# Four gathers of expert outputs, spread over the last item of a mixture-of-experts layer

## The reference

```
def moe_swiglu(h, router, w1, w3, w2):
    ...
    top_val, top_idx = lax.top_k(logits, TOP_K)          # two experts for each token
    gates = jax.nn.softmax(top_val, axis=-1)
    ...
    def one_block(args):
        xi, e = args
        return (jax.nn.silu(xi @ w1[e]) * (xi @ w3[e])) @ w2[e]

    yb = lax.map(one_block, (xb, block_e)).reshape(cap, D)
    out = jnp.zeros_like(t).at[slot_tok].add(yb * slot_g[:, None].astype(yb.dtype))
```

## Time and profile before

| | |
|---|---|
| median of three runs | 1869.29 us |
| the profiled execution's own time | 1876.34 us |
| its span | 1874.5 us |
| PE busy | 1820.3 us (97%) |
| DVE busy | 1383.7 us (74%) |
| ACT busy | 1119.5 us (60%) |
| POOL busy | 191.2 us (10%) |
| HBM read | 475.05 MB |
| DMA, whole span | 265 GB/s |

### The profile page before, as it was taken

How to read it: one execution, slowest core, us unless ns; L and a number is a source line. 1 busy time by engine, 2 the same in 40 slices (tenths; PEclk the granted TensorE clock), 3 DMA queues, 4 the chain that set the end, 5 groups by cost and what they waited for, 6 DMA issues and landing times.

```text
span 1874.5 us, 25088 instructions
## 1 busy us (share of the span) xinstructions
PE 1820.3 (97%) x8832; PEld 1455.8 (78%) x8832; DVE 1383.7 (74%) x1738; ACT 1119.5 (60%) x1531; POOL 191.2 (10%) x253
## 2 busy tenths in 40 slices
PE   5999989999999999999999999999999999999998
PEld 2777657888888887658888888888888888888886
DVE  2534586787646664543898998999988999898896
ACT  2423484422222223474688877788877888877784
POOL 0116331011001101530100000000000000000002
PEclk8899999999999999999999999999999999999999
DMA  9354401597555451130999999999999999999995
GB/s 355 120 180 155 149 1 50 198 326 266 170 180 180 162 174 43 63 118 1 330 386 362 383 377 368 392 380 383 386 353 383 372 384 393 355 390 380 374 377 192
DMA packets 234932, 496.42 MB, mean 265 GB/s; under 512 B 6128, under 2 KB 44016, under 8 KB 234864
## 3 DMA queue, kind: packets, MB, share of 16 engines
q1 hardware_dynamic: 231328, 488.53, 71.3%
q0 software_dynamic: 1920, 5.77, 0.9%
q10 hardware_dynamic: 1616, 1.22, 0.2%
HBM read 475.05 MB, written 20.45 MB: 264 GB/s over the span
## 4 chain that ended last, share of the span: by engine, by line
PE 82%; DMA 6%; DVE 5%; ACT 3%; issue 2%; POOL 1%; SPq 1%; DVEq 0%; ACTq 0%; POOLq 0%
PE ps L2373 9%; PE ps L2375 9%; PE ps L2374 9%; PE ps L2179 7%; PE ps L2181 6%; PE ps L2180 6%; PE ps L2387 5%; PE ps L2385 5%; PE ps L2386 5%; DMA ring<-in_moe_w 5%; PE ps L1974 2%; PE ps L2030 2%; PE ps L1976 2%; PE ps L1975 2%; PE ps L2051 2%
## 5 line engine op out<-in xcount | busy, mean ns | idle before, releaser
L1752 DVE TENSOR_TENSOR wlo<-ring,whi 128x1024 fp32r<-128x1024 f32 x672 | 793.8, 1226 | 91.1 <-ACT whi L1257 83.3
L1257 ACT ACTIVATE whi<-ring 128x1024 fp32r<-128x1024 f32 x672 | 686.4, 1056 | 185.3 <-DMA ring<-in_moe_w 98.0
L2373 PE MATMUL ps<-whi,xgr 128*128 128x512 f32 x896 | 353.5, 394 | 0.1
L2375 PE MATMUL ps<-whi,xgr 128*128 128x512 f32 x896 | 349.4, 390 | 0.0
L2374 PE MATMUL ps<-wlo,xgr 128*128 128x512 f32 x896 | 348.7, 389 | 0.0
L1174 ACT ACTIVATE fsa<-ring 128x1024 fp32r<-128x1024 f32 (+2 forms) x73 | 68.8, 943 | 255.6 <-PE ps L2181 254.2
L2375 PEld LDWEIGHTS ps<-whi,xgr 128*128 128x128 f32 x896 | 168.2, 188 | 35.8
L2373 PEld LDWEIGHTS ps<-whi,xgr 128*128 128x128 f32 x896 | 168.3, 188 | 33.8 <-issue 0.5
L2374 PEld LDWEIGHTS ps<-wlo,xgr 128*128 128x128 f32 x896 | 168.4, 188 | 33.6
L2385 PE MATMUL ps<-whi,hidr 128*128 128x512 f32 x448 | 176.9, 395 | 0.0
L2387 PE MATMUL ps<-whi,hidr 128*128 128x512 f32 x448 | 175.3, 391 | 0.0
(11 more groups left out here) (324 smaller groups left out, 2739.1 us busy)
## 6 DMA issues: line engine op xcount, KB each, us to landing
ring<-in_moe_w SPq DMA_DIRECT2D x168, 2048.0 KB, 9.9
ring<-in_ada_w SPq DMA_DIRECT2D x24, 2048.0 KB, 8.4
ring<-in_ev_w_in SPq DMA_DIRECT2D x6, 2048.0 KB, 8.0
ring<-in_ffn_w_gate SPq DMA_DIRECT2D x11, 1024.0 KB, 5.6
ring<-in_ffn_w_up SPq DMA_DIRECT2D x11, 1024.0 KB, 8.2
expert_tokens<-scr SPq DMA_DIRECT2D x4, 1536.0 KB, 14.6
ring<-in_ffn_w_down SPq DMA_DIRECT2D x4, 1536.0 KB, 6.6
ring<-in_ffn_w_down SPq DMA_DIRECT2D x4, 1280.0 KB, 6.1
```

The costliest lines, as they stand in the source:

```text
L1257: act.activation(whi[:, u % URING, :], mslot[(u // 4) % MRING][:, (u % 4) * UNIT:(u % 4 + 1) * UNIT], ACT.Copy).then_inc(m_hi, 1)
L1752: dve.tensor_tensor(wlo[:, u % URING, :], mslot[(u // 4) % MRING][:, (u % 4) * UNIT:(u % 4 + 1) * UNIT], whi[:, u % URING, :].bitcast(F32) ...
L2373: pe.matmul(bank[:, :], xgr[:, 0, kk, :], hi[:, ws], start=(kk == 0), stop=False)
L2375: ins = pe.matmul(bank[:, :], xgr[:, 1, kk, :], hi[:, ws], start=False, stop=(kk == KT - 1))
```

## The change

Each of the four fetches gets a wait of its own: the k-th (k = 0 to 3) waits for what also releases the load of chunk 9 + 3k, that is the low parts of units 27, 39, 51 and 63. The scalings move from ACT's steps 73, 74, 75, 76 to steps 40, 47, 58, 70. The turns on PE move from behind units 76 and 80 to behind units 67 and 75. Nothing is computed otherwise.

```
@@ pool @@
             pool.wait_ge(y_st, last_n * 16 + 16)
-            pool.wait_ge(m_lo, last_n * NU + (LO0 + 4 * (MCH - 1 - MRING) + 4))
-            pool.sem_inc(y_all, 1)
-            pool.wait_ge(y_all, 1)
             pool.wait_ge(xs_rd, 64)
             pool.wait_ge(bidx_rd, 1)
             for t in range(2):
                 for c in range(2):
+                    pool.wait_ge(m_lo, last_n * NU + (LO0 + 4 * (9 + 3 * (2 * t + c) - MRING) + 4))
+                    pool.sem_inc(y_all, 1)
+                    pool.wait_ge(y_all, 2 * t + c + 1)
                     pool.indirect_dma_start(pick[c][t], None, ys,
@@ act @@
-                    if last and h in (73, 74, 75, 76):
-                        t, c = (h - 73) // 2, (h - 73) % 2
+                    if last and h in (40, 47, 58, 70):
+                        t, c = h // 50, (40, 47, 58, 70).index(h) % 2
                         act.wait_ge(bidx_rd, 1)
                         act.wait_ge(pick_rd[t], 32)
@@ pe @@
-                    if last and h in (76, 80):
-                        turn_choices((h - 76) // 4)
+                    if last and h in (67, 75):
+                        turn_choices((h - 67) // 8)
```

## The result

| | before | changed |
|---|---|---|
| median (9 runs each) | 1869.8 us | 1878.86 us |
| lowest to highest | 1867.63 to 1874.92 | 1872.85 to 1884.74 |
| profiled execution, own time | 1876.34 | 1884.74 |
| first to last unit of the last item (start of unit 0 to start of unit 83) | 126.48 | 137.05 |

The ratio is 1.0042, with a 95% interval of 1.0027 to 1.0057: 7.9 us slower, 5.0 to 10.7. The forecast was 5.8 us slower.

A forecast was written before the change was run, and what follows sets the result against it. PE's 4.10 us wait for POOL's first sum and the half clock after it bound the last item. 12.9 added less 7.06 removed gave +5.8 us, 1875.0 us after carrying over the profile's offset; range 1864.5 to 1881.5.

The forecast's parts named there:

- The wait at step 58: ACT's third scaling waits for the fourth fetch, making PE 9.75 us late at unit 65; 12.9 us with clock and 0.15.
- The landing: Time from a fetch's issue on POOL until its data arrive: taken as 9.5 us, with ends of 5.6 and 13.2.
- step 40: ACT's second scaling waits about 3 us for the second fetch; unit 47 is ready at 1806.4, wanted at 1806.62.
- the pause behind unit 51: PE waits 2.3 us at the transposes there for DVE's late product; counted as part of the next term.
- The bandwidth: Three fetches ahead of unit 63's low part make it 3.8 us late, with 0 and 4.2 as bounds.
- The clock: Half clock for 5.9 us after PE's long pause ahead of unit 65 costs 2.96 us, as in the kernel before.
- The second sum: POOL's sum of 2.35 us ends near 1859, before PE is behind unit 75 at 1861; costed at nothing.
- That cover is thin, 2 us: The reserve between the end of POOL's second sum, near 1859, and PE's arrival behind unit 75 at 1861.
- Removed, 7.06 us: PE's wait of 4.10 us behind unit 76 for POOL's first sum goes, with 2.96 us of half clock.
- Rival A: Fetches land in 5.6 us, PE is 3.5 us late without low clock: 3.5 us faster, 1865.8; chance 0.14.
- Rival B: Fetches land in 13.2 us, unit 47 also 3.45 us late: 12.1 us slower, 1881.4; chance 0.18.

The follow-up runs named there:

- the three fastest kernels: Changed kernel with scalings 68, 69, turn 82: 0.9982; before with turns 81, 83: 0.9979; changed with fourth fetch at chunk 15, second scaling at 50: 0.9979.

## Why the prediction was right, and where it was not

**The wait at step 58: right.** The forecast had ACT wait about 10 us, PE 7.4 us in one pause and unit 65 at 9.75 us late. Measured: 10.24, and 7.15. Counted from unit 0, unit 65 started at 102.71 us (1839.74 - 1737.03) instead of 92.82 (1832.05 - 1739.23), 9.9 late. In the second profiled executions it was 8.8 (100.5 and 91.8 us after unit 0). Where the 7.15 us come from can be read off: when unit 63's low part was done (1826.16), PE had 6.4 us of work left before unit 65 (to 1832.59), and issue, landing, scaling and the two parts of unit 65 took 13.6 (to 1839.74). The kernels that keep the wait pause there for 6.4 to 7.2 us, but for the one with work put into the pause; the four that avoid it, by a later use or an earlier fetch, do not pause there.

**The landing: right for the fourth fetch, the one that decides.** Forecast 9.5 us; the fetches took 8.0, 8.0, 9.8 and 9.3. With the second at 8.0, ACT waited 1.46 us at step 40, not 3, and the pause behind unit 51 was 0.58 us, not 2.3. In this trace no packet of a fetch ran for the first 4.3 to 5.4 us after its issue, so about half of its time is over before one of its bytes moves. The estimate of 4.5 us from issue, made from the fit in the Trainium skill ("DMA: Bandwidth & Descriptors", section "Anatomy of one DMA — SWDGE (gpsimd) path") and POOL's instruction, is not what a fetch took here beside a DMA share of 1.02: over all the kernels they took 7.0 to 10.2.

**The bandwidth: the term was too large, and its agreement is luck.** Unit 63's low part was ready 89.1 us after unit 0 (1826.16 - 1737.03) instead of 84.8, 4.3 later, where I had 3.8. But 1.0 of that was there at unit 27's low part (36.1 instead of 35.1), ahead of the first fetch. Over all profiled executions unit 63's low part came at 85.4 to 89.1, 86.5 on average, in the eight with three fetches ahead of it, and at 83.3 to 85.8, 84.6 on average, in the three with none. That is 1.9 us, half of the term. The median landing of a weight chunk went from 10.3 to 10.9 us. The seven buffers and PE's reserve absorb it: with no wait on a fetch, PE loses 0.3 us.

**The clock: the term was mis-sized.** I took 2.96 us, from how long PE was slow after it resumed. In the first profiled execution of the changed kernel it was 1.45, in the second 1.95, as the windows there have half clock from 1836.6 to 1843.4 and PE is back at 1839.51. The slow stretches are of the same length in all three, 6.8 us; after the pause of 4.10 us 0.9 of it lay inside the pause, with those of 6.40 and 7.15 us 2.9 and 3.9, where it costs nothing.

**The second sum, with "That cover is thin, 2 us": the step that failed.** The forecast priced it at nothing, as one high part, a scaling and a sum of 2.35 us were to end 2 us before PE came. The price of the sum was that of the kernel before, where DVE had gaps. The cover was even larger than forecast: the sum began at 1851.76 and PE came at 1857.65, so one of 2.4 us had 3.5 us to spare. It took 9.22 us beside DVE at full work in one execution, 3.19 in another. When it is long, it adds 6.2 us. The trace of before had a sign of it that I did not use: DVE's low parts beside the two sums took 2.5 and 3.0 us instead of 1.2.

**Removed, 7.06 us:** the size read is that of the one execution; it was 5.6 in the other.

**How much of the number is luck.** Forecast +5.8, measured +7.9 (5.0 to 10.7). The sign and the place of the loss rest on the wait at step 58, which the runs show. The size is a sum of errors that partly cancel: bandwidth and clock were each too large by 1 to 2 us, the loss removed by up to 1.5, and the second sum too small by 0 or 6.2.

**Rival A** (fetches light, faster) fails on the landing, 9.3 us for the fourth where it needed 5.6. **Rival B** (landings over 9.8 us and a failure at step 40) did not come: PE did not wait for unit 47.

## What to carry to other kernels

- Moving a transfer earlier is free only with its first reader. Ask what the reader's engine has queued behind the wait, and at which point of the pipeline the *last* transfer that it waits for is released: here one semaphore counted two fetches, and the reader of the first stood for the second.
- Lead time must be counted from the release to the step, in the time of the full system (7 to 10 us, five to seven units here), and be set against the work that PE still has when the release comes: 6.4 us here, under five units.
- An elementwise sum on POOL is not free cover beside a busy DVE. Place it behind what PE needs from DVE next, and leave room for it to take longer than alone, up to four times here.

## What the runs showed of the hardware that I had not expected

**POOL and DVE exclude each other, and a busy DVE can keep POOL out for long.** POOL's sum of two 128 x 1024 tiles took 2.3 to 2.9 us where it began first or DVE had a gap. Where DVE made low parts one behind the other it took 9.22 us in one execution and 3.19 in another. A low part that lost to a sum took up to 3.8 us instead of 1.22. The Trainium skill, "SBUF — State Buffer", section "Who interferes with whom", says that a DVE instruction with two inputs in SBUF and a POOL instruction that reads SBUF take turns for whole instructions, and that the one that starts first blocks the other. The trace agrees, and shows more: blocked by one low part, POOL was passed by six others before its turn came (9.22 - 2.39 = 6.8 us, six low parts of 1.14). Why it came at once in the other execution (3.19 us, DVE as busy) no run here shows.

**Work put into a pause need not save the clock.** With 2.5 us of idling in place of 7.15 it fell to 0.50 all the same, and for 6.8 us. In the kernel with the fourth fetch at chunk 15 a pause of 3.65 us was followed by a slow stretch half as long, 3.4 us:

```profile
1815.00:1818.00 3.00, 3.00 (x9) 2.34 (x8) 3.00 (x4) 0.96 (x2) 0.00 (x0) 0.50 0.93 306
1818.00:1820.00 2.00, 2.00 (x9) 1.59 (x8) 2.00 (x3) 1.36 (x3) 0.00 (x0) 0.89 1.01 416
```

In the three fastest kernels, whose pauses stay at 1.1 us or less, the last item has no such stretch.
